# A two-layer hybrid decoder in split float32: the sixteen k tiles of the transposed activations laid 1056 bytes apart instead of 1024

## What is computed

```python
D_MODEL = 2048; SEQ = 256; DEPTH = 2; D_FF = 5632; ALPHA = (2 * DEPTH) ** 0.25

def conv_ffn(x, w_up, conv_w, conv_b, w_down):
    h = x @ w_up                               # (256, 2048) @ (2048, 11264)
    h = causal_depthwise_conv3(h, conv_w) + conv_b
    g, u = h[..., :D_FF], h[..., D_FF:]
    return (jax.nn.silu(g) * u) @ w_down       # (256, 5632) @ (5632, 2048)

for i in range(DEPTH):
    y = swa_sink_attention(x, ...) if i % 2 == 0 else forgetting_attention(x, ...)
    x = layer_norm(ALPHA * x + y, ln_g[i, 0], ln_b[i, 0])
    y = conv_ffn(x, ffn_w_up[i], ffn_conv_w[i], ffn_conv_b[i], ffn_w_down[i])
    x = layer_norm(ALPHA * x + y, ln_g[i, 1], ln_b[i, 1])
```

## The kernel before, in words

| tensor | begins at | modulo 512 | step from tile to tile |
|---|---|---|---|
| ident | 16512 | 128 | - |
| w_hi | 51200 | 0 | blocks of 512 bytes |
| w_lo | 67584 | 0 | blocks of 512 bytes |
| xh | 104448 | 0 | 1024 |
| xl | 120832 | 0 | 1024 |
| oh, hid_h | 137216 | 0 | 1024 |
| hid_l | 182272 | 0 | 1024 |
| qT, kz | 182272, 186368 | 0 | 1024 |
| wf_hi | 214208 | 192 | 128 |
| wf_lo | 216256 | 192 | 128 |

## Time and profile before

### The profile page before, as it was taken

The page is one execution under the profiler, slowest core; times in us unless marked ns, Lnnn a source line. Parts: engine busy times, 40 slices in busy tenths (PEclk is TensorE's granted clock), DMA queues, the critical chain, the costliest instruction groups (busy, mean ns, idle before and its releaser), DMA issues.

```text
span 2237.8 us, 40894 instructions
## 1 busy us (share of the span) xinstructions
PE 2207.8 (99%) x15265; PEld 2061.6 (92%) x15265; DVE 1337.7 (60%) x1805; ACT 1038.4 (46%) x1380; POOL 217.1 (10%) x206
## 2 busy tenths in 40 slices
PE   9999999999999999999999999999999999999996
PEld 8998899999999988888999998899999999988885
DVE  5566676665666554546665565576666566554445
ACT  4554464454444443335444444364444444443332
POOL 2000002220000000000240330001230000000001
PEclk9999999999999999999999999999999999999998
DMA  8444556666666666655655654656666666666653
GB/s 263 148 147 159 178 170 198 190 194 182 183 180 185 179 193 192 195 190 163 189 182 163 201 169 141 204 155 196 193 199 182 180 185 179 185 225 191 194 193 109
DMA packets 206953, 408.71 MB, mean 183 GB/s; under 512 B 12653, under 2 KB 13757, under 8 KB 206621
## 3 DMA queue, kind: packets, MB, share of 16 engines
q1 hardware_dynamic: 200192, 385.92, 56.8%
q0 software_dynamic: 5776, 21.34, 3.0%
q10 hardware_dynamic: 908, 0.43, 0.1%
HBM read 405.46 MB, written 2.18 MB: 182 GB/s over the span
## 4 chain that ended last, share of the span: by engine, by line
PE 96%; DVE 3%; ACT 0%; issue 0%; DMA 0%; DVEq 0%; ACTq 0%
PE ps L1178 19%; PE ps L1181 19%; PE ps L1180 19%; PE ps L1164 11%; PE ps L1166 11%; PE ps L1165 11%; PE ps L1306 1%; PE ps L1313 1%; PE ps L1325 1%; PE ps L1324 1%; PE ps L1305 1%; DVE w_lo L751 1%; PE ps L1323 0%; PE ps L1255 0%; DVE cg L796 0%
## 5 line engine op out<-in xcount | busy, mean ns | idle before, releaser
L751 DVE TENSOR_TENSOR w_lo<-raw,w_hi 128x1024 fp32r<-128x1024 f32 x728 | 922.5, 1273 | 672.7 <-ACT w_hi L473 671.1
L473 ACT ACTIVATE w_hi<-raw 128x1024 fp32r<-128x1024 f32 x728 | 770.3, 1058 | 999.7 <-PE ps L1181 582.5
L1178 PE MATMUL ps<-xh,w_lo 128*128 128x256 f32 x3572 | 1020.0, 286 | 2.5 <-DVE xl L792 1.5
L1181 PE MATMUL ps<-xh,w_hi 128*128 128x256 f32 x3572 | 1010.6, 283 | 0.0
L1180 PE MATMUL ps<-xl,w_hi 128*128 128x256 f32 x3572 | 1010.5, 283 | 0.0
L1178 PEld LDWEIGHTS ps<-xh,w_lo 128*128 128x128 f32 x3572 | 685.0, 192 | 5.4 <-DVE xl L792 2.9
L1180 PEld LDWEIGHTS ps<-xl,w_hi 128*128 128x128 f32 x3572 | 685.2, 192 | 0.3
L1181 PEld LDWEIGHTS ps<-xh,w_hi 128*128 128x128 f32 x3572 | 685.0, 192 | 0.0
L1164 PE MATMUL ps<-w_lo,hid_h 128*128 128x512 f32 x704 | 273.9, 389 | 0.0
L1165 PE MATMUL ps<-w_hi,hid_l 128*128 128x512 f32 x704 | 273.9, 389 | 0.0
L1166 PE MATMUL ps<-w_hi,hid_h 128*128 128x512 f32 x704 | 273.9, 389 | 0.0
(11 more groups left out here) (164 smaller groups left out, 1497.1 us busy)
## 6 DMA issues: line engine op xcount, KB each, us to landing
raw<-in_ffn_w_up_dram SPq DMA_DIRECT2D x352, 512.0 KB, 3.6
raw<-in_ffn_w_down_dram SPq DMA_DIRECT2D x176, 512.0 KB, 4.6
raw<-in_b_w_qkvf_dram SPq DMA_DIRECT2D x96, 512.0 KB, 4.4
raw<-in_a_w_qkv_dram SPq DMA_DIRECT2D x40, 512.0 KB, 4.4
raw<-in_a_w_o_dram SPq DMA_DIRECT2D x32, 512.0 KB, 4.3
raw<-in_b_w_o_dram SPq DMA_DIRECT2D x32, 512.0 KB, 4.6
bias<-rel_by_distance POOLq DMA_DIRECT2D x4, 1024.0 KB, 6.4
bias<-minus_cumulated_decay POOLq DMA_DIRECT2D x4, 1024.0 KB, 6.4
```

What stands on the lines that cost most here:

```text
L473: act.activation(w_hi[:, loc % RING], raw[:, loc % RING], ACT.Copy).then_inc(high_ready, 1)
L751: dve.tensor_tensor(w_lo[:, s], raw[:, s], w_hi[:, s].bitcast(FP32), ALU.subtract).then_inc(low_ready, 1)
L1178: pe.matmul(o, w_lo[:, slot, k % 2, cols], xh[:, k, :], start=(k == 0 and j % 2 == 0), stop=False, skip_group_check=True)
L1181: last = pe.matmul(o, w_hi[:, slot, k % 2, cols], xh[:, k, :], start=False, stop=(k == KT - 1), skip_group_check=True)
```

## The change

The rows of `xh` and `xl` are allocated 264 elements long and used to 256. So k tile k begins 1056k bytes behind the tensor's start instead of 1024k, that is 32k bytes past a multiple of 512 (0, 32, 64, up to 480), and no two of the sixteen stand at the same place within 512 bytes. `xl` now begins at 121344 (modulo 512: 0), and everything behind it lies 1024 bytes further on, with the same remainders modulo 512. `w_hi`, `w_lo`, `xh`'s own start and all that lies ahead of it stay.

```diff
 MT = SEQ // P
+ROW = SEQ + 8
...
         with ExitStack() as first:
-            xh = sb("xh", [P, KT, SEQ], F32R, first)
+            xh = sb("xh", [P, KT, ROW], F32R, first)[:, :, 0:SEQ]
         with ExitStack() as later:
             lnfull = sb("lnfull", [P, 2, D], FP32, later)
-        xh_hold = sb("xh_hold", [P, KT * SEQ])
-        xl = sb("xl", [P, KT, SEQ], F32R)
+        xh_hold = sb("xh_hold", [P, KT * ROW])
+        xl = sb("xl", [P, KT, ROW], F32R)[:, :, 0:SEQ]
```

## The result

The changed kernel takes 2223.7 us (median of 3 runs, 2223.45 to 2223.86) against 2239.02: 15.3 us less, a ratio of 0.9931 with a 95% interval of 0.9908 to 0.9953. Its profiled execution took 2223.86 us with a span of 2222.1, 15.7 us less than the span before.

The account below looks back on a forecast made before the run. PE was taken as the bound, through the distance between its matmul starts. The profiled 2239.63 us plus terms of 0, with the runs' median 0.6 us below that execution, gave 2239.0 us; range 2204 to 2274.

Parts of the forecast that it names:

- likeliest case: Whole kernel: no effect beyond 0.2%, chance 0.53, the time lying between 2235 and 2243 us.
- What bounds the kernel: Up-projections: PE has no idle time, so a change of the distance between two matmuls goes into the time one to one.
- Readers on TensorE, the count: Matmuls reading xh or xl: 11,280, of which 15/16, 10,575, read from a new place; 10.6 us per nanosecond.
- What a new place costs: 0 ns: Matmuls reading xh or xl off a multiple of 512: no change in distance, taken from the two nearest rows.
- my two rows: Forget gates' stationary tiles at four places, 113.3 ns throughout; float32 identity moving from 128 modulo 512, remainder 2.7 ns.
- The bounds, 6.7 ns either way: Matmuls reading from a new place: remainder varies by 13.3 against 6.6 ns, so 71 us less or more.
- Writers, shifted tensors: Writes of xh and xl in two runs of 256: cost 0, at most 0.6 us; tensors moved 1024 bytes: 0.
- Rival A: TensorE: next load and running matmul meet in memory, so new places make it faster; 71 us in full; chance 0.20.
- A's price of 35 us at half: Rival A with 3.3 ns given back per matmul: 35 us less, 2204 us.
- Its sign, 120 ns at tile 0: Rival A in the changed profile: over 1669 starts per window, distance differing by k tile and 120 at tile 0.
- Rival B: Turned products: a start off 512 slows the moving fp32r stream; 2274 us at half, 2310 in full; chance 0.27.

Follow-up runs that it names:

- the two mixed runs: Against the kernel before: rows of 264 in xh alone, 2226.61 us; xh begun 192 bytes past a multiple of 256 with xl on one, 2232.51 us.
- the run at 192: Kernel before with xh and xl both begun 192 bytes past a multiple of 512, all else keeping its place modulo 512: executions from 2176.46 to 2214.27 us.
- the relation 96: Kernel before with xh and xl both begun 96 bytes past a multiple of 512, the weights unmoved: 2242.75 us, ratio 1.0016.

## Why the prediction was right in its range and wrong in its likeliest case

*What bounds the kernel.* Right. The time is the distance between PE's starts; 15.5 of 15.7 us are found there, and no new bound came even at 113.3 ns, where the DMA share rose to 0.66.

*Readers on TensorE, the count.* Right with one flaw: I left tile 0 out since it doesn't move. Its distance fell as well, to 119.0, and as the two mixed runs show, a matmul's distance depends on its neighbours too.

*What a new place costs: 0 ns.* This step failed. I judged places one by one, by the remainder modulo 512, where it is the relation of two operands modulo 256. Read so, my two rows said nothing of the case. The identity on itself has both operands at one place, relation 0, as everything else had. The forget gates' "four different places" are two relations only, 64 and 192, taken in turn, and with the 32-column load both leave a single step, as 0 and 128 do. They then rose to 116.4 when the moving tiles took eight relations. For the turned stream a new place is worth 1.7 ns in the mean of the changed kernel, and from 0 to 6.7 ns where all tiles share one relation.

*The bounds, 6.7 ns either way.* The lower bound is reached: 13.3 against 6.6 ns of remainder are two steps against one, and the run at 192 gets from 120.0 to 113.3 in its best execution. The changed kernel gets a quarter of that. That the bound came from the gates was luck in part, since they have their 6.6 ns from the shorter load. The upper bound was not approached: no relation that was run keeps the turned stream above 120.0.

*Writers, shifted tensors.* Right: L792 and L523 kept 690 and 633 ns, the down-projections their 273.9 us. One reading was off: the two groups of L891 in the earlier trace rows are 10 and 6 writes and don't part the backward ones from the others. The 16 writes singly do, and they agree: 679 to 693 ns for layer 0's eight, 680 to 692 for layer 1's.

*Rival A* is what happened, at 0.20: where the two operands stand to each other sets the distance. Its evidence (6.6 ns left where the load begins elsewhere) was no evidence, since the gates have 113.3 ns at a relation of 0 and 128 as well; the objection to it, that the length of the load counts there, was right for the gates. What went wrong is that it was then carried over to the 128-column load, where the place does count. A's price of 35 us at half was the right order for a single well-chosen place; the spread gave 15.3. Its sign, 120 ns at tile 0, failed by 1 ns. Its mechanism, two reads that meet, fits the relation, the period and the steps of 16 columns, but no run shows the meeting itself.

*The rule of the Trainium skill* ("TensorE: Matmul & The Clock Gate", Part 2, Step-by-step) that loading the next weights takes nothing from the running matmul would give one distance for all relations. The runs have 113.3 to 120.0 ns for one and the same instructions by where their operands lie, so the measurement decides against it for these fp32r streams: load and running matmul are not independent of each other. By what they hinder each other isn't shown.

*Rival B.* Its sign is real elsewhere: products with `xh` stationary and 512 columns moving lost 5.7 ns each, and the relation 96 is 3.5 us slower than 0 in all. For the turned stream it is out.

*The numbers.* 2239.0 forecast, 2223.7 measured, inside 2204 to 2274. The likeliest case's own range, 2235 to 2243, was missed. The wide range holds because it had room for half of A's price; the forecast itself rests on the 0 ns that failed.

## What to carry to other kernels

When a dense stream of matmuls with a weight load each runs at one distance to the nanosecond, and that is longer than its columns take, try moving one operand's tensor by 64 to 224 bytes against the other's, in several steps, before rewriting anything (96 bytes gave nothing here). In this kernel a filler of 192 bytes, with one behind `xl` that puts the rest back, is worth 25 to 63 us, four times the change studied in its best execution, and it needs no longer rows. Compare distances between starts (the count in a window of fixed length), since busy time and clock look perfect all along. Check both kinds of product, as the place that helps one with 256 moving columns can hurt one with 512, and take several executions, since one program can settle in more than one pattern.

## What was not expected of the hardware

- The relation counts modulo 256 bytes: 0 and 256 both give 120.00 ns, and moving both operands alike changes nothing (2240.1 us with everything moved by 192).
- Distances settle to whole 16-column steps over patterns of 1 to 9 matmuls: 17 steps (113.33 ns) at best, 18 (120.00) at worst, 119.26, 119.17, 118.67, 118.33, 117.78, 117.33 between. All this is for 256 moving columns, a load of 128 columns before each matmul, and the clock at full.
- At a relation of 192 one program has two patterns, 113.33 and 117.78 ns, keeps one through a whole up-projection of some 500 us, and takes from 2176.5 to 2214.3 us at one and the same clock.
- The short load of the forget gates (32 columns) leaves 113.3 ns at relations of 0 and 128 as well as 64 and 192.
- 16 bytes matter: 208 gives 119.17 ns beside the 117.78 or 113.33 at 192.
- Open: a relation of 32 for the turned stream, a way to make the 113.33 ns pattern certain, and by what mechanism the place of a load acts on the running matmul. No run was made for these.
